# A mixture-of-experts encoder layer: experts with one block and with two taken in turn, in an order worked out on the chip

## The chip, the cores and the metric

The kernel runs on one core of one Trainium2 chip. The metric is the device time of one execution in microseconds (us). The engines are PE (TensorE: matrix products), DVE (VectorE), ACT (ScalarE), POOL (GpSimd) and SP (SyncE, which here only issues transfers); 16 DMA engines move data between HBM and the on-chip memories SBUF and PSUM.

## The reference

1024 tokens of width 1024 pass one layer: an RMSNorm, one projection `w_in`, two mixing branches (a spatial gating and a real 2-D Fourier transform), an output projection and the residual; then the experts, and a last RMSNorm. The part that matters here:

```
hn = rms_norm(h, norm2_g)
scores = sigmoid(hn @ w_router)                     # 64 experts
eidx, gates = top 8 of 64 per token, from the best 4 of 8 groups of experts
for every expert e: rows that chose it, padded to blocks of 128:
    out = (silu(xb @ w_gate[e]) * (xb @ w_up[e])) @ w_down[e] * gate
    y[tok] += out
h = h + y + shared expert(hn)
```

`w_gate[e]` and `w_up[e]` are 1024 x 256 and `w_down[e]` is 256 x 1024, all float32: 3 MB an expert, 192 MB for the 64. How many rows choose an expert depends on the input. With the inputs of the reference its routing gives every expert between 71 and 238 rows: 35 experts have up to 128 rows and so one block, 29 have more and so two, 93 blocks in all.

## The kernel before

**Three stages.** Up to about 345 us the dense part runs (projections, mixing, output projection, router scores). From there to about 457 us the tables of the experts are made, beside the shared expert. Then the expert stage takes the 93 blocks, here called items, one after the other, and after it the copies of the result are added and normalised.

**Tables (L1204 to L1282, L640 to L705).** DVE counts each expert's blocks (`nch`), PE adds them up over the experts with a triangular matrix (L688), and DVE derives for every item its expert and whether it is the first item of that expert. PE transposes these two columns (L692) and DVE writes them as rows 0 and 1 of `tab` (L1255, semaphore `s_tab`). Then for each of eight chunks of 128 tokens `slot_marks(c)` on DVE makes 8 `mark` and 8 `pick` tiles (L1263, L1265) in one of two buffers, and `table(c)` on PE multiplies them into the table of row numbers (L665); so `slot_marks(c)` waits for `table(c-2)`. Meanwhile PE does the shared expert: `s_gate_up(q, j)` (L648, eight pieces of 8 products) and `s_down(c)` (L658, eight pieces), with `shared_h(q)` on DVE between (L1137). `s_down(0)` waits for all four `shared_h` (semaphore `s_hm`). When the last `table` is through, DVE makes `idx_all` and `row_all` (L1280, L1282), which POOL's gathers wait for, and then takes the sums `y0(c)` (L1334); `s_down(c)` waits for `y0(c-2)`.

**Weights.** An expert's float32 weights are loaded by SP (L281, L282, L285) to `raw_gu` and `raw_dn`, each with two places. ACT makes a rounded copy (`split_gu`, L919, four parts; `split_dn`, L923, two parts), DVE the rest of it (`rest_gu`, L1144; `rest_dn`, L1151), into `w_gu` and `w_dn`, also with two places, taken in turn. Place 0 of `w_gu` lies where `xh` lies, from which `y0` is stored, so it is filled only after these stores. SP's order is fixed, whatever the blocks are: gate and up of expert e+1 (after expert e-1's are split), wait until expert e's have landed, down of expert e, wait for the landing of down of e-1, and on (L370 to L420). The loads of experts 0 and 1 are issued as soon as the output projection is done (L360), at about 347 us.

**One item i.** PE: transposes the gathered rows of i+1 (L464), `down(i-1)` (L735, 12 products), transposes h of i (L743), `gate_up(i+1)` (L721, 24 products). ACT and DVE do in item i: silu and gating, the two halves of the transposed rows (L934, L1297), and under `If`: the split of gate and up of the expert whose first item is i+2, and the split of down of the expert whose first item is i+1. So the weights are split at a fixed distance of items, and a place of `raw_gu` comes free two items before its expert is used. POOL gathers rows four items ahead (L1464), copies the gates (L1474) and adds the results to memory (L1492). Engines read `tab` into registers with `look` (L304), a `TENSOR_LOAD` and some register instructions.

Experts are taken by their number. With S for an expert of one item and D for one of two, this order is D S D D S S S D S D S D D S S D S S S S S D D D D D D D S S S S D S S D D D D S S S S S S S S D D D D S D S D S S D D D S S S S.

Of the kernel before, what the change touches and what calls it, by code (L numbers as in the profile page):

```python
# [31 lines left out]
NE = 64  # L32
# [5 lines left out]
KF = F // P  # L38
# [4 lines left out]
TAB = NITEM + 8  # L43
# [4 lines left out]
TURN = 3  # L48
GU_PARTS = 4
# [13 lines left out]
def build(nc, x, g1, w_in, ln_g, ln_b, wsT, bsT, ga, gb, w_out, g2, w_router, rbias, wg, wu, wd,  # L63
          sg, su, sd, dft_pos, dft_ch, gf, out, hn_d, y_d):
    ctx = ExitStack()
    with ctx:
        top = [nc.sbuf_base]

        def place(name, shape, dt, at=None):

            size = 2 if dt in (BF16, F16) else 4
            n = size
            for s in shape[1:]:
                n *= s
# [120 lines left out]
        tab = place("tab", [2, TAB], I32)  # L195
# [18 lines left out]
        def sem(name):  # L214
            return ctx.enter_context(nc.semaphore(name))
# [99 lines left out]
        def _(sp):  # L315
# [42 lines left out]
                sp.dma_start(hn_v[c, :, 0:D], rows[:, c % 2, :]).then_inc(s_hst[c % 2], 16)  # L358

            sp.wait_ge(s_wo, NC)  # L360
            for e in range(2):
                load_gu(sp, e, 1 - e)
                load_dn(sp, e, 1 - e)

            sp.wait_ge(s_gates, 1)
            sp.dma_start(gates_v[:, :, D:], rt_a[:, :, :]).then_inc(s_gst, 16)
            sp.wait_ge(s_gu_in[1], 32)
            sp.sem_inc(s_rg, 1)

            def load_next_gu(e, at):  # L370
                sp.wait_ge(s_hg, (e - 1) * GU_PARTS)
                sp.sem_inc(s_turn_sp, 1)
                sp.wait_ge(s_lg, (e - 1) * GU_PARTS)
                sp.sem_inc(s_turn_sp, 1)
                load_gu(sp, e, at)

            def load_next_dn(e, at):
                sp.wait_ge(s_hd, (e - 1) * KF)
                sp.sem_inc(s_turn_sp, 1)
                sp.wait_ge(s_ld, (e - 1) * KF)  # L380
                sp.sem_inc(s_turn_sp, 1)
                load_dn(sp, e, at)

            def gu_landed(at, fills):

# [74 lines left out]
        def _(pe):  # L460
# [223 lines left out]
            mm.then_inc(s_pm, 1)  # L684
            s_gate_up(0, 1)

            pe.wait_ge(s_chunks, 1)
            pe.matmul(ps[6][:, 0:NE], nchb[:, :], triI[:, :], start=True, stop=True).then_inc(s_pm, 1)  # L688
            s_gate_up(1, 0)

            pe.wait_ge(s_cols, 1)
            pe.matmul(ps[7][0:2, 0:P], cols[:, 0:2], ident[:, :], start=True, stop=True).then_inc(s_pm, 1)  # L692
            s_gate_up(1, 1)
            s_gate_up(2, 0)
            table(0)
            table(1)
            s_gate_up(2, 1)
            table(2)
            table(3)
            s_gate_up(3, 0)  # L700
            table(4)
            table(5)
            s_gate_up(3, 1)
            table(6)
            table(7)  # L705

            def turn_item(u, fills):

# [293 lines left out]
        def _(dv):  # L1002
# [218 lines left out]
            shared_h(0)

            dv.wait_ge(s_pm, 2)
            step(dv.tensor_copy(le[:, 2, :], ps[6][:, 0:NE]))
            step(dv.tensor_scalar(le[:, 0, :], le[:, 2, :], pidx[:, 0:1], None, ALU.is_le))
            step(dv.tensor_tensor(le[:, 1, :], le[:, 0, :], le[:, 2, :], ALU.mult))
            step(dv.tensor_reduce(cols[:, 2:3], le[:, 0, :], AX.X, ALU.add))
            step(dv.tensor_reduce(cols[:, 3:4], le[:, 1, :], AX.X, ALU.max))
            step(dv.tensor_scalar(cols[:, 0:1], cols[:, 2:3], float(NE - 1), None, ALU.min))
            step(dv.tensor_scalar(cols[:, 4:5], cols[:, 3:4], pidx[:, 0:1], None, ALU.is_equal))  # L1230
            step(dv.tensor_scalar(cols[:, 5:6], cols[:, 2:3], float(NE), None, ALU.is_lt))
# [4 lines left out]
            step(dv.tensor_scalar(ends[0:1, 0:1], ps[6][0:1, NE - 1:NE], 1.0, 1.0 / TURN, ALU.add, ALU.mult))  # L1236
# [4 lines left out]
            many((dv.memset(le[:, 3, 0:1], 0.0),  # L1241
                  dv.tensor_scalar(le[:, 3, 1:NE], le[:, 2, 0:NE - 1], float(P), None, ALU.mult)))
# [8 lines left out]
            many((dv.tensor_scalar(ends[:, 3:4], le[:, 2, NE - 1:NE], 1.0, 1.0 / TURN, ALU.add, ALU.mult),))  # L1251
            step(dv.tensor_copy(late[:, :], ends[:, 3:4]))
            step(dv.tensor_scalar(late[:, :], late[:, :], 1.0, float(TURN), ALU.subtract, ALU.mult))
            dv.wait_ge(s_pm, 3)
            dv.tensor_copy(tab[0:2, 0:P], ps[7][0:2, 0:P]).then_inc(s_tab, 1)  # L1255

            dv.wait_ge(s_info, 3)

            def slot_marks(c):

# [118 lines left out]
        def _(gp):  # L1379
# [205 lines left out]
```

## Time and profile before

| | us |
|---|---|
| three runs | 1404.11, 1408.82 (median), 1414.78 |
| the profiled execution, its own time | 1411.65 |
| its span, from the first to the last instruction | 1410.0 |
| busy in it: PE, DVE, ACT, POOL | 1309.5, 875.7, 738.1, 459.0 |

The span lies 1.65 us under the execution's own time. The profile's page lists busy times and the costliest groups of instructions; the chain of waits follows the work that ended last back from the end, in pieces; a piece such as "PE ps L721 x24" is a whole gate_up of one item. Stretches give busy times and DMA share between two times of the span.

### The profile page before, as it was taken

How to read it: one execution, taken by the hardware profiler on the slowest of the kernel's cores; microseconds unless marked ns; L12 is line 12 of the kernel's file. 1: busy time of each engine (PE TensorE's matmuls, PEld its weight loads, DVE VectorE, ACT ScalarE, POOL GpSimd, SP SyncE). 2: the span in 40 equal slices, each digit the busy share in tenths (PEclk: the TensorE clock that was granted, in tenths of full speed). 3: DMA queues.
4: the chain of work that ended last, by engine and by line, in shares of the span. 5: the costliest groups of instructions: out<-in, count | busy, mean ns of one | idle time of the engine just before them, and what ended most of it. 6: DMA issues, size and time to landing. Idle time of an engine off the chain costs nothing.

```text
span 1410.0 us, 25859 instructions
## 1 busy us (share of the span) xinstructions
PE 1309.5 (93%) x5960; PEld 1024.4 (73%) x5962; DVE 875.7 (62%) x1318; ACT 738.1 (52%) x1044; POOL 459.0 (33%) x608
## 2 busy tenths in 40 slices
PE   6899988999999999999989999999999999999960
PEld 5785466888444887888878888788877788888850
DVE  4430444345665676767866567776687666775846
ACT  4421244211011676767865657766677666775822
POOL 1431201000001344434443344334343434443435
PEclk9999999999999999999999999999999999999985
DMA  9464032002306799999999889999899989999987
GB/s 336 150 180 160 0 119 90 40 36 80 152 5 241 248 302 340 327 305 326 339 365 280 259 250 318 363 344 282 253 366 376 325 249 306 325 339 278 295 257 279
DMA packets 99535, 348.47 MB, mean 247 GB/s; under 512 B 13104, under 2 KB 33584, under 8 KB 82736
## 3 DMA queue, kind: packets, MB, share of 16 engines
q1 hardware_dynamic: 72144, 263.64, 48.7%
q0 software_dynamic: 27360, 84.44, 26.4%
q8 instruction: 16, 0.26, 0.1%
q14 instruction: 15, 0.12, 0.0%
HBM read 294.85 MB, written 71.57 MB: 260 GB/s over the span
## 4 chain that ended last, share of the span: by engine, by line
PE 71%; DMA 14%; ACT 3%; issue 3%; DVE 2%; POOL 1%; DVEq 1%; ACTq 1%; SPq 0%; POOLq 0%
PE ps L721 26%; PE ps_out L735 13%; DMA raw_gu<-in_w_up 8%; PE ps L613 6%; PE ps L481 5%; PE ps L464 5%; DMA raw_dn<-in_w_down 5%; PE ps L648 4%; PE ps L515 4%; PE ps L564 2%; ACT w_gu L919 1%; DMA y_rows_dram<-ob,idxs 1%; PE ps_out L630 1%; PE ps L743 1%; PE ps L658 1%
## 5 line engine op out<-in xcount | busy, mean ns | idle before, releaser
L721 PE MATMUL ps<-w_gu,xTh 128*128 x1504 | 477.9, 399 | 13.2 <-DVE xTl L1297 11.1
L1144 DVE TENSOR_TENSOR w_gu<-raw_gu,w_gu (+1 forms) x256 | 302.6, 1223 | 63.8 <-ACT w_gu L919 62.9
L721 PEld LDWEIGHTS ps<-w_gu,xTh 128*128 128x128 f32 x1504 | 279.0, 190 | 73.5 <-issue 19.3
L721 PE MATMUL ps<-w_gu,xTl 128*128 x752 | 296.6, 394 | 0.0
L919 ACT ACTIVATE w_gu<-raw_gu (+1 forms) x256 | 256.8, 1060 | 23.7 <-SPq L387 23.7
L735 PE MATMUL ps_out<-w_dn,hTh 128*128 x744 | 242.1, 407 | 0.0
L1492 POOL DMA_INDIRECT y_rows_dram<-ob,idxs x93 | 151.7, 1632 | 194.8 <-ACT ob L940 175.9
L1151 DVE TENSOR_TENSOR w_dn<-raw_dn,w_dn (+1 forms) x128 | 150.9, 1221 | 84.0 <-ACT w_dn L923 83.6
L721 PEld LDWEIGHTS ps<-w_gu,xTl 128*128 128x128 f32 x752 | 142.6, 190 | 30.0
L735 PEld LDWEIGHTS ps_out<-w_dn,hTh 128*128 128x128 f32 x744 | 133.1, 189 | 25.1
L735 PE MATMUL ps_out<-w_dn,hTl 128*128 x372 | 145.9, 392 | 0.0
L923 ACT ACTIVATE w_dn<-raw_dn (+1 forms) x128 | 128.4, 1057 | 31.8 <-SPq L391 31.6
L1297 DVE TENSOR_TENSOR xTl<-ps,xTh 128x512 fp32r<-128x512 f32 x188 | 120.9, 685 | 26.0 <-ACT xTh L934 26.0
L1464 POOL DMA_INDIRECT Xg<-hn_rows_dram,idxg x97 | 105.7, 1089 | 79.0 <-POOL idxg L1461 76.9
L1474 POOL COPY gate<-Xg 128x1 f32 x94 | 37.4, 398 | 287.6 <-PE ps L464 166.0
L934 ACT ACTIVATE xTh<-ps 128x512 fp32r<-128x512 f32 x188 | 102.3, 597 | 51.5 <-PE ps L464 51.5
L929 ACT ACTIVATE hs<-ps 128x256 f32<-128x256 f32 x93 | 35.7, 384 | 151.4 <-PE ps L721 151.0
L464 PEld LDWEIGHTS ps<-ident,Xg 128*128 128x128 f32 x752 | 98.0, 190 | 8.1 <-issue 0.5
L1412 POOL TENSOR_SCALAR rs<-ms 128x1 f32<-128x1 f32 x40 | 25.8, 645 | 239.9 <-ACT junk L789 238.3
L940 ACT ACTIVATE ob<-ps_out 128x1024 f32<-128x1024 f32 x93 | 95.1, 1022 | 7.0 <-PE ps_out L735 7.0
L464 PE MATMUL ps<-ident,Xg 128*128 128x128 f32 x752 | 98.3, 274 | 0.0
L1290 DVE SCALAR_TENSOR_TENSOR hh<-hs,gate,ps 128x256 f32<-128x256 f32 x93 | 44.6, 479 | 63.3 <-ACT hs L929 44.0
(206 smaller groups left out, 1554.8 us busy)
## 6 DMA issues: line engine op xcount, KB each, us to landing
raw_gu<-in_w_gate SPq DMA_DIRECT2D x64, 1024.0 KB, 7.5
raw_gu<-in_w_up SPq DMA_DIRECT2D x64, 1024.0 KB, 10.8
raw_dn<-in_w_down SPq DMA_DIRECT2D x64, 1024.0 KB, 14.8
y_rows_dram<-zero SPq DMA_DIRECT2D x1, 9216.0 KB, 37.6
x_ring<-in_x SPq DMA_DIRECT2D x8, 512.0 KB, 5.0
w_in_sb<-in_w_in SPq DMA_DIRECT2D x8, 512.0 KB, 9.7
xh<-in_x SPq DMA_DIRECT2D x8, 512.0 KB, 8.2
w_out_sb<-in_w_out SPq DMA_DIRECT2D x1, 4096.0 KB, 12.9
```

Source lines behind the costliest of these rows:

```text
L464: last = pe.transpose(ps[banks[k // 4]][:, (k % 4) * P:(k % 4 + 1) * P], src[:, k:D:KD], ident[:, :])
L721: mm = pe.matmul(ps[3][:, :], x_[:, k, :], w_gu[:, bass.ds(at, 1), part, :, k, :], start=(k == 0 and part == 0 and x_ is xTh), stop=(k == ...
L735: mm = pe.matmul(ps[6 + half][:, :], h_[:, k, :], w_dn[:, bass.ds(at, 1), part, k, half * 512:(half + 1) * 512], start=(k == 0 and part == ...
L919: act.activation(gu_part(w_gu[:, :, 0, :, :, :], at, m), gu_part(raw_gu, at, m), ACT.Copy).then_inc(s_hg, 1)
L923: act.activation(w_dn[:, bass.ds(at, 1), 0, k, :], raw_dn[:, bass.ds(at, 1), k, :], ACT.Copy).then_inc(s_hd, 1)
L934: act.activation(xTh[:, half * 4:half * 4 + 4, :], ps[1 + half][:, :].rearrange("p (k t) -> p k t", k=4), ACT.Copy).then_inc(s_xa, 1)
L940: act.activation(ob[:, u, :], ps_out[:, :], ACT.Copy).then_inc(s_oa, 1)
L1144: dv.tensor_tensor(gu_part(w_gu[:, :, 1, :, :, :], at, m), gu_part(raw_gu, at, m), gu_part(w_gu[:, :, 0, :, :, :], at, m).bitcast(F32), AL ...
L1151: dv.tensor_tensor(w_dn[:, bass.ds(at, 1), 1, k, :], raw_dn[:, bass.ds(at, 1), k, :], w_dn[:, bass.ds(at, 1), 0, k, :].bitcast(F32), ALU.s ...
L1297: dv.tensor_tensor(xTl[:, part, :], ps[1 + half][:, :].rearrange("p (k t) -> p k t", k=4), xTh[:, part, :].bitcast(F32), ALU.subtract).the ...
L1464: gp.indirect_dma_start(out=Xg[:, u, :], out_offset=None, in_=hn_d[:, :], in_offset=bass.IndirectOffsetOnAxis(ap=idxg[:, u:u + 1], axis=0) ...
L1492: gp.indirect_dma_start(out=y_d[:, :], out_offset=bass.IndirectOffsetOnAxis(ap=idxs[:, u:u + 1], axis=0), in_=ob[:, u, :], in_offset=None, ...
```

## The change

The order of the experts is worked out on the chip. DVE marks which experts have more than one block (`multi`), PE sums these marks, and DVE makes a key per expert that spreads both kinds evenly (`key_t`, `kinds`), and from the keys a matrix `upto` of who comes before whom, which takes the place of the triangular one. `tab` gets a third row, the number of the expert in place j. SP looks there before each load, and POOL looks there for the column of the gate, behind its look at row 0. All else goes by place j instead of expert e. For the inputs of the reference the order becomes

S D S D S D S D S D S S D S D S D S D S D S S D S D S D S D S S D S D S D S D S D S S D S D S D S D S D S S D S D S D S D S D S

with five places where two S stand together, and no two D together. Since the loads need row 2 of `tab`, those of the first two experts now wait for `s_tab`. PE's small products of the tables and the pieces of the shared expert stand in another order, and `shared_h(3)` on DVE stands ahead of the wait for the last table.

```
--- before.py
+++ after.py
             sp.wait_ge(s_wo, NC)
-            for e in range(2):
-                load_gu(sp, e, 1 - e)
-                load_dn(sp, e, 1 - e)
-
             sp.wait_ge(s_gates, 1)
             sp.dma_start(gates_v[:, :, D:], rt_a[:, :, :]).then_inc(s_gst, 16)
+            sp.wait_ge(s_tab, 1)
+            for j in range(2):
+                e = look(sp, 2, j, NE - 1)
+                load_gu(sp, e, 1 - j)
+                load_dn(sp, e, 1 - j)
...
-                load_gu(sp, e, at)
+                load_gu(sp, look(sp, 2, j, NE - 1), at)
...
-                load_dn(sp, e, at)
+                load_dn(sp, look(sp, 2, j, NE - 1), at)
...
+            pe.wait_ge(s_kinds, 1)
+            pe.matmul(ps[6][:, 0:NE], multi[:, :], tri[0:NE, 0:NE], start=True, stop=True)
+            pe.matmul(ps[6][:, NE:2 * NE], multi[:, :], identb[:, :], start=True, stop=True)
+            pe.matmul(ps[6][:, 2 * NE:2 * NE + 1], multi[:, :], ones[0:NE, 0:1], start=True, stop=True).then_inc(s_pm, 1)
+            s_gate_up(1, 0)
+
             pe.wait_ge(s_chunks, 1)
-            pe.matmul(ps[6][:, 0:NE], nchb[:, :], triI[:, :], start=True, stop=True).then_inc(s_pm, 1)
-            s_gate_up(1, 0)
+            pe.matmul(ps[7][:, 0:NE], nchb[:, :], upto[:, :], start=True, stop=True)
+            pe.matmul(ps[7][:, NE:2 * NE], nchb[:, :], identb[:, :], start=True, stop=True)
+            pe.matmul(ps[7][:, 2 * NE:3 * NE], ones[0:NE, :], upto[:, :], start=True, stop=True)
+            pe.matmul(ps[7][:, 3 * NE:3 * NE + 1], nchb[:, :], ones[0:NE, 0:1], start=True, stop=True).then_inc(s_pm, 1)
+            s_gate_up(1, 1)
...
-            for c in range(4):
+            s_down(0)
+            s_down(1)
+            table(6)
+            table(7)
+            for c in range(2, 6):
                 s_down(c)
             turn_item(0, 1)
-            for c in range(4, NC):
+            for c in range(6, NC):
                 s_down(c)
...
+            step(dv.tensor_tensor(identb[:, :], triI[:, :], tri[0:NE, 0:NE], ALU.subtract))
+            step(dv.tensor_scalar(pidx1[:, :], pidx[:, :], 1.0, None, ALU.add))
             dv.wait_ge(s_pm, 1)
+            step(dv.tensor_scalar(multi[:, :], ps[5][0:NE, 0:1].to_broadcast([NE, P]), float(P), None, ALU.is_gt))
+            dv.sem_inc(s_kinds, 1)
...
+            dv.wait_ge(s_pm, 2)
+            before, is_multi = ps[6][0:NE, 0:NE], ps[6][0:NE, NE:2 * NE]
+            n_multi, n_single = kinds[:, 0:1], kinds[:, 1:2]
...
+            many((dv.tensor_scalar(key_t[:, 0, :], key_t[:, 0, :], 0.5, n_multi, ALU.add, ALU.mult),
+                  dv.tensor_scalar(key_t[:, 1, :], before, 0.5, n_single, ALU.add, ALU.mult)))
...
+            step(dv.tensor_scalar(upto[:, :], key_t[:, 0, :], kinds[:, 3:4], None, ALU.is_ge))
+            dv.sem_inc(s_chunks, 1)
             shared_h(0)
...
+            shared_h(3)
             dv.wait_ge(s_table, NC)
...
             dv.tensor_tensor(row_all[:, :], idx_all[:, :], copy_row[:, :], ALU.add).then_inc(s_idx, 1)
-            shared_h(3)
...
-                e = look(gp, 0, i, NE - 1)
+                e = look(gp, 2, look(gp, 0, i, NE - 1), NE - 1)
```

PE, from the last small product of the tables to the first pieces of `s_down`, before (L648 is `s_gate_up`, L665 `table`, L658 `s_down`; a row of L665 x16 is two tables):

```order
L692 MATMUL ps_out<-ident,cols 2x128
L648 MATMUL ps<-T,sgu_w 128x512 x16
L665 MATMUL ps<-mark,pick 128x136 x16
L648 MATMUL ps<-T,sgu_w 128x512 x8
L665 MATMUL ps<-mark,pick 128x136 x16
L648 MATMUL ps<-T,sgu_w 128x512 x8
L665 MATMUL ps<-mark,pick 128x136 x16
L648 MATMUL ps<-T,sgu_w 128x512 x8
L665 MATMUL ps<-mark,pick 128x136 x16
L658 MATMUL ps<-sd_w,hsT 128x512 x4
L658 MATMUL ps_out<-sd_w,hsT 128x512 x4
```

The same place on PE after the change (L656, L673 and L666 are the same three functions):

```order
L709 MATMUL ps_out<-ident,cols 3x128
L656 MATMUL ps<-T,sgu_w 128x512 x16
L673 MATMUL ps<-mark,pick 128x136 x16
L656 MATMUL ps<-T,sgu_w 128x512 x8
L673 MATMUL ps<-mark,pick 128x136 x16
L656 MATMUL ps<-T,sgu_w 128x512 x8
L673 MATMUL ps<-mark,pick 128x136 x16
L666 MATMUL ps<-sd_w,hsT 128x512 x4
L666 MATMUL ps_out<-sd_w,hsT 128x512 x4
L673 MATMUL ps<-mark,pick 128x136 x16
L666 MATMUL ps<-sd_w,hsT 128x512 x4
L666 MATMUL ps_out<-sd_w,hsT 128x512 x4
```

The first pair of tables stands behind six of the eight pieces of `s_gate_up` instead of five; the last pair, which stood ahead of `s_down(0)`, stands behind `s_down(1)`, and no `s_gate_up` is left beside the last two `slot_marks`.

DVE, from the third `shared_h` (L1137) to the first `y0` (L1334), before:

```order
L1137 TENSOR_TENSOR hsT<-s_tmp,ps 128x512
L1263 TENSOR_SCALAR mark<-count_row,item_110,token 128x136 x8
L1265 TENSOR_SCALAR pick<-count_row,place_111 128x128 x8
L1263 TENSOR_SCALAR mark<-count_row,item_110,token 128x136 x8
L1265 TENSOR_SCALAR pick<-count_row,place_111 128x128 x8
L1277 TENSOR_SCALAR late_row<-count_row,late 128x136
L1278 TENSOR_TENSOR copy_row<-copy_row,late_row 128x136
L1280 TENSOR_SCALAR idx_all<-ps,dump 128x136
L1282 TENSOR_TENSOR row_all<-idx_all,copy_row 128x136
L1137 TENSOR_TENSOR hsT<-s_tmp,ps 128x512
L305 TENSOR_LOAD tab
L305 ISA x2
```

And after (L1155 is `shared_h`):

```order
L1155 TENSOR_TENSOR hsT<-s_tmp,ps 128x512
L1304 TENSOR_SCALAR mark<-count_row,item_110,token 128x136 x8
L1306 TENSOR_SCALAR pick<-count_row,place_111 128x128 x8
L1304 TENSOR_SCALAR mark<-count_row,item_110,token 128x136 x8
L1306 TENSOR_SCALAR pick<-count_row,place_111 128x128 x8
L1318 TENSOR_SCALAR late_row<-count_row,late 128x136
L1319 TENSOR_TENSOR copy_row<-copy_row,late_row 128x136
L1155 TENSOR_TENSOR hsT<-s_tmp,ps 128x512
L1322 TENSOR_SCALAR idx_all<-ps,dump 128x136
L1324 TENSOR_TENSOR row_all<-idx_all,copy_row 128x136
L312 TENSOR_LOAD tab
L312 ISA x2
```

The last `shared_h` moved ahead of `idx_all`, and still stands behind `slot_marks(6)` and `slot_marks(7)`.

## Rows read from the trace of the kernel before

**Rows 1.** The page: busy us of each engine, and one group of instructions (mean ns).

```profile
PE 1309.5 (93%) x5960; PEld 1024.4 (73%) x5962; DVE 875.7 (62%) x1318; ACT 738.1 (52%) x1044; POOL 459.0 (33%) x608
...
L1144 DVE TENSOR_TENSOR w_gu<-raw_gu,w_gu (+1 forms) x256 | 302.6, 1223 | 63.8 <-ACT w_gu L919 62.9
```

**Rows 2.** The chain of waits, expert stage: start us, us, what.

```profile
457.69 7.12 PE ps L721 x24
...
751.26 5.48 PE ps L721 x24
...
863.76 5.48 PE ps L721 x24
...
1010.76 5.46 PE ps L721 x24
...
1048.19 14.98 DMA raw_gu<-in_w_up
...
1117.00 5.74 PE ps L721 x24
...
1345.08 5.71 PE ps L721 x24
```

**Rows 3.** The chain of waits, where one and two items alternate.

```profile
565.76 5.50 PE ps L721 x24
...
575.17 5.73 PE ps L721 x24
...
594.19 5.46 PE ps L721 x24
...
613.24 5.46 PE ps L721 x24
...
1239.71 5.48 PE ps L721 x24
...
1259.10 5.48 PE ps L721 x24
```

**Rows 4.** Stretches: start:end length, busy of PE PEld DVE ACT POOL, PEclk, DMA share, GB/s.

```profile
565.00:622.00 57.00, 56.95 (x279) 47.15 (x278) 40.52 (x48) 38.47 (x53) 23.99 (x31) 1.00 0.97 311
751.00:864.00 113.00, 113.00 (x557) 94.36 (x556) 68.94 (x85) 69.45 (x99) 44.88 (x61) 1.00 0.89 262
1027.00:1113.00 86.00, 79.30 (x367) 64.29 (x366) 65.32 (x76) 62.34 (x83) 32.46 (x40) 0.96 1.03 370
```

**Rows 5.** Timeline, making the tables, PE, DVE: start us, us, engine, line.

```profile
393.05 1.11 PE L665 MATMUL ps<-mark,pick 128*128 128x136 f16 x16
393.73 1.89 DVE L1263 TENSOR_SCALAR mark<-count_row,item,token 128x136 f16<-128x136 f16 x8 [5.76 <-PE ps L665]
...
397.08 1.89 DVE L1263 TENSOR_SCALAR mark<-count_row,item,token 128x136 f16<-128x136 f16 x8 [0.16 <-DVE pick L1265]
...
418.27 0.30 DVE L1282 TENSOR_TENSOR row_all<-idx_all,copy_row 128x136 int32<-128x136 int32 x1
418.48 0.68 DVE L1137 TENSOR_TENSOR hsT<-s_tmp,ps 128x512 f32<-128x512 f32 x1
...
419.31 1.10 PE L658 MATMUL ps<-sd_w,hsT 128*128 128x512 f32 x2 [1.56 <-DVE hsT L1137]
```

**Rows 6.** The chain of waits from the last y0 to the first hh.

```profile
447.94 1.30 DVE xh L1334 x2
...
449.26 4.68 DMA y_rows_dram<-xh
...
454.99 0.31 DVEq L305
...
455.34 0.18 DVEq L305
```

**Rows 7.** Timeline of ACT and of DVE, a D behind an S.

```profile
606.51 2.01 ACT L923 ACTIVATE w_dn<-raw_dn  x2 [1.62 <-SPq L391]
...
610.89 0.69 DVE L1297 TENSOR_TENSOR xTl<-ps,xTh 128x512 fp32r<-128x512 f32 x1 [0.20 <-ACT xTh L934]
```

More of the change, by code:

```diff
@@ L168, in build @@
         gidx = place("gidx", [P, NC, 8], U32, M_AT + 3 * KB + 256)
+        key_t = place("key_t", [NE, 4, NE], F32, M_AT)
+        multi = place("multi", [NE, P], BF16, M_AT + 3 * KB + 768)
         late_row = place("late_row", [P, TAB], F32, M_AT + 3 * KB)
@@ L194, in build @@
         cols = place("cols", [P, 12], F32)
-        tab = place("tab", [2, TAB], I32)
+        tab = place("tab", [3, TAB], I32)
+        identb = place("identb", [NE, NE], BF16)
+        upto = place("upto", [NE, NE], BF16)
+        kinds = place("kinds", [NE, 4], F32)
+        pidx1 = place("pidx1", [P, 1], F32)
         ends = place("ends", [P, 8], I32)
@@ L246, in build @@
         s_mask, s_chunks, s_cols = sem("mask_ready"), sem("chunks_ready"), sem("item_cols_ready")
+        s_kinds = sem("kinds_ready")
         s_rv, s_pm, s_tab = sem("routing_step"), sem("routing_matmul"), sem("tables_ready")
@@ L685, in _ @@
             s_gate_up(0, 1)
-            pe.wait_ge(s_chunks, 1)
-            pe.matmul(ps[6][:, 0:NE], nchb[:, :], triI[:, :], start=True, stop=True).then_inc(s_pm, 1)
-            s_gate_up(1, 0)
+            pe.wait_ge(s_kinds, 1)
[3 more added lines that the diff above has]
+            s_gate_up(1, 0)
+            pe.wait_ge(s_chunks, 1)
+            pe.matmul(ps[7][:, 0:NE], nchb[:, :], upto[:, :], start=True, stop=True)
[3 more added lines that the diff above has]
+            s_gate_up(1, 1)
             pe.wait_ge(s_cols, 1)
-            pe.matmul(ps[7][0:2, 0:P], cols[:, 0:2], ident[:, :], start=True, stop=True).then_inc(s_pm, 1)
-            s_gate_up(1, 1)
+            pe.matmul(ps[6][0:3, 0:P], cols[:, 0:3], ident[:, :], start=True, stop=True).then_inc(s_pm, 1)
             s_gate_up(2, 0)
+            s_gate_up(2, 1)
             table(0)
             table(1)
-            s_gate_up(2, 1)
+            s_gate_up(3, 0)
             table(2)
             table(3)
-            s_gate_up(3, 0)
+            s_gate_up(3, 1)
             table(4)
             table(5)
-            s_gate_up(3, 1)
-            table(6)
-            table(7)
             def turn_item(u, fills):
@@ L1220, in _ @@
             dv.wait_ge(s_t3, NC)
+            dv.wait_ge(s_info, 3)
+            dv.wait_ge(s_pm, 2)
+            before, is_multi = ps[6][0:NE, 0:NE], ps[6][0:NE, NE:2 * NE]
+            n_multi, n_single = kinds[:, 0:1], kinds[:, 1:2]
+            many((dv.tensor_scalar(n_multi, ps[6][0:NE, 2 * NE:2 * NE + 1], 1.0, None, ALU.max),
+                  dv.tensor_scalar(kinds[:, 2:3], ps[6][0:NE, 2 * NE:2 * NE + 1], -1.0, float(NE), ALU.mult, ALU.add),
+                  dv.tensor_tensor(key_t[:, 0, :], count_row[0:NE, 0:NE], before, ALU.subtract)))
@@ new lines, in _ @@
+            step(dv.tensor_scalar(n_single, kinds[:, 2:3], 1.0, None, ALU.max))
+            many((dv.tensor_scalar(key_t[:, 0, :], key_t[:, 0, :], 0.5, n_multi, ALU.add, ALU.mult),
+                  dv.tensor_scalar(key_t[:, 1, :], before, 0.5, n_single, ALU.add, ALU.mult)))
+            step(dv.scalar_tensor_tensor(out=key_t[:, 1, :], in0=key_t[:, 1, :], scalar=0.25, in1=key_t[:, 0, :],
+                                         op0=ALU.add, op1=ALU.subtract))
+            step(dv.tensor_tensor(key_t[:, 1, :], key_t[:, 1, :], is_multi, ALU.mult))
@@ L1221, in _ @@
+            step(dv.tensor_tensor(key_t[:, 0, :], key_t[:, 0, :], key_t[:, 1, :], ALU.add))
+            step(dv.tensor_tensor(key_t[:, 2, :], key_t[:, 0, :], ident[0:NE, 0:NE], ALU.mult))
+            step(dv.tensor_reduce(kinds[:, 3:4], key_t[:, 2, :], AX.X, ALU.add))
+            step(dv.tensor_scalar(upto[:, :], key_t[:, 0, :], kinds[:, 3:4], None, ALU.is_ge))
+            dv.sem_inc(s_chunks, 1)
             shared_h(0)
-            dv.wait_ge(s_pm, 2)
-            step(dv.tensor_copy(le[:, 2, :], ps[6][:, 0:NE]))
+            dv.wait_ge(s_pm, 3)
@@ L1225, in _ @@
+            step(dv.tensor_copy(le[:, 2, :], ps[7][:, 0:NE]))
             step(dv.tensor_scalar(le[:, 0, :], le[:, 2, :], pidx[:, 0:1], None, ALU.is_le))
             step(dv.tensor_tensor(le[:, 1, :], le[:, 0, :], le[:, 2, :], ALU.mult))
+            step(dv.tensor_reduce(cols[:, 8:9], le[:, 0, :], AX.X, ALU.add))
+            step(dv.scalar_tensor_tensor(out=le[:, 0, :], in0=ps[7][:, 2 * NE:3 * NE], scalar=pidx1[:, 0:1],
+                                         in1=count_row[:, 0:NE], op0=ALU.is_equal, op1=ALU.mult))
@@ L1227, in _ @@
             step(dv.tensor_reduce(cols[:, 2:3], le[:, 0, :], AX.X, ALU.add))
             step(dv.tensor_reduce(cols[:, 3:4], le[:, 1, :], AX.X, ALU.max))
-            step(dv.tensor_scalar(cols[:, 0:1], cols[:, 2:3], float(NE - 1), None, ALU.min))
+            step(dv.tensor_scalar(cols[:, 0:1], cols[:, 8:9], float(NE - 1), None, ALU.min))
             step(dv.tensor_scalar(cols[:, 4:5], cols[:, 3:4], pidx[:, 0:1], None, ALU.is_equal))
-            step(dv.tensor_scalar(cols[:, 5:6], cols[:, 2:3], float(NE), None, ALU.is_lt))
+            step(dv.tensor_scalar(cols[:, 5:6], cols[:, 8:9], float(NE), None, ALU.is_lt))
@@ L1235, in _ @@
             dv.sem_inc(s_cols, 1)
-            step(dv.tensor_scalar(ends[0:1, 0:1], ps[6][0:1, NE - 1:NE], 1.0, 1.0 / TURN, ALU.add, ALU.mult))
+            step(dv.tensor_scalar(ends[0:1, 0:1], ps[7][0:1, 3 * NE:3 * NE + 1], 1.0, 1.0 / TURN, ALU.add, ALU.mult))
             many((dv.tensor_scalar(ends[0:1, 1:2], ends[0:1, 0:1], 1.0, None, ALU.subtract),
@@ L1239, in _ @@
                   dv.tensor_scalar(ends[0:1, 4:5], ends[0:1, 0:1], 2.0, None, ALU.subtract)))
-            many((dv.memset(le[:, 3, 0:1], 0.0),
-                  dv.tensor_scalar(le[:, 3, 1:NE], le[:, 2, 0:NE - 1], float(P), None, ALU.mult)))
+            step(dv.tensor_tensor(le[:, 3, :], le[:, 2, :], ps[7][:, NE:2 * NE], ALU.subtract))
+            step(dv.tensor_scalar(le[:, 3, :], le[:, 3, :], float(P), None, ALU.mult))
             step(dv.scalar_tensor_tensor(out=rt_b[:, :, :], in0=ps[4][:, :].rearrange("p (c e) -> p c e", c=NC),
@@ L1250, in _ @@
                                          op0=ALU.mult, op1=ALU.add))
-            many((dv.tensor_scalar(ends[:, 3:4], le[:, 2, NE - 1:NE], 1.0, 1.0 / TURN, ALU.add, ALU.mult),))
+            many((dv.tensor_scalar(ends[:, 3:4], ps[7][:, 3 * NE:3 * NE + 1], 1.0, 1.0 / TURN, ALU.add, ALU.mult),))
             step(dv.tensor_copy(late[:, :], ends[:, 3:4]))
             step(dv.tensor_scalar(late[:, :], late[:, :], 1.0, float(TURN), ALU.subtract, ALU.mult))
-            dv.wait_ge(s_pm, 3)
-            dv.tensor_copy(tab[0:2, 0:P], ps[7][0:2, 0:P]).then_inc(s_tab, 1)
-            dv.wait_ge(s_info, 3)
+            dv.wait_ge(s_pm, 4)
+            dv.tensor_copy(tab[0:3, 0:P], ps[6][0:3, 0:P]).then_inc(s_tab, 1)
             def slot_marks(c):
```

13 lines of the change are left out of this document (6 added, 7 removed).

## The prediction

> **What bounds the kernel now.** I read the page first: PE is busy for 1309.5 us of 1410.0, DVE for 875.7 [rows 1]. So a gain must come from PE's waits, and next I looked for them in the chain of waits, whose pieces "PE ps L721 x24" are one gate_up per item. The expert stage runs from the gate_up of item 1 at 457.69 to that of item 92 at 1345.08: 887.39 us for 91 items [rows 2]. In the run of seven D, 12 items take 863.76 - 751.26 = 112.50 us, 9.375 each: this is PE's own pace, with matmuls and nothing else in the chain. 91 items at that pace are 853.1 us, so 34.3 us of the stage are waits. The reader is to see where: from 1010.76 to 1117.00, the end of a D and the eight S behind it, ten items take 106.24 us instead of 93.75, 12.5 too many, and there a DMA of 14.98 us on raw_gu stands in the chain [rows 2]. An S asks for 3.15 MB of weights in 9.4 us, a D in 18.8.
>
> The stretches say the same of the DMA engines [rows 4]: 370 GB/s at a share of 1.03 in the run of S, 262 at 0.89 in the run of D, 311 at 0.97 where they alternate. From the run of D, 262 GB/s x 18.75 us = 4.91 MB a D, of which 1.77 belong to the rows of two items, 0.885 each. A pair S D then moves 6.29 + 3 x 0.885 = 8.95 MB; at the 370 GB/s of the run of S that is 24.2 us, while PE needs 28.1 for its three items. So an alternating order should be bound by PE. Where before it does alternate, the trace agrees: an S and the D behind it take 594.19 - 565.76 = 28.43 us, 0.30 over three paces, the gate_up at 575.17 lasting 5.73 instead of 5.46 [rows 3].
>
> **The expert stage after.** There are 29 D; the first holds items 1 and 2, and 28 follow an S behind item 2. Terms:
> - 91 items at 9.375: 853.1 us.
> - The gate_up at 457.69 takes 7.12 us instead of 5.5 [rows 2]; PE had waited before it. It stays: 1.6.
> - The 0.30 us of a D behind an S. I put it on DVE: where both split jobs fall in one item there are six parts of 1.22 us [rows 1], two xTl of 0.69 [rows 7], and hh and hTl of some 0.45, together 9.6 us against a pace of 9.375. The change keeps it: 28 x 0.30 = 8.4.
> - Two S together, five places. The one at 1239.71 has the same neighbours (S D S S D); its two items take 19.39 us to 1259.10 [rows 3], 0.64 over two paces, so 0.34 more than the usual 0.30: 5 x 0.34 = 1.7.
> - SP's new looks. One costs 0.31 + 0.18 us with its gaps, 0.53, on DVE [rows 6]; SP's is not shown. The loads that have slack hide it. The tight one is the down of a D behind an S, for which ACT waits: at 606.51 it is released by SP's landing [rows 7]. SP issues this down just after the next gate and up, so it queues behind 2 MB in the same queue, and I count one look, not two. There the second xTl ends near 612.2 and PE wants it at 613.24 [rows 3, 7], so here 0.53 us would be hidden. Bounds per D: 0, and 1.06 if both looks reach PE; nearest to the row is 0, but landings vary, so I take 0.15: 4.2.
> Sum 869.0 us, against 887.4: 18.4 us saved. POOL's second look costs nothing here: it falls where POOL waits for PE's transposes. ACT, PE and DVE look at rows 0 and 1 as before.
>
> By the Trainium skill, "DMA: Bandwidth & Descriptors", section "Latency and other measured facts", loading registers has a floor near 600 ns. The look of 0.53 us on DVE lies a little under it; at 0.6 the 4.2 us of the looks would become at most some 2 us more.
>
> **The start of it.** Here the change costs time, on PE's path.
> - Small products: seven and one more stop for three and a wait. They delay the last s_gate_up by about 1.3 us (bounds 0.5 and 3), and the next term starts from that one's end, so they count in full.
> - s_down(0) waits for the last shared_h, which DVE does behind slot_marks(6) and (7). Before, these two ran beside the last s_gate_up, since the tables stood one piece of it earlier. Now slot_marks(6) starts only behind table(4), itself behind the last s_gate_up. A table pair to its mark is 393.73 - 393.05 = 0.7 us, a slot_marks is 397.08 - 393.73 = 3.35 [rows 5]. So from the start of the last pair before s_down: 0.7 + 2 x 3.35 + 0.65 (late_row, copy_row) + 0.85 (shared_h and its semaphore, 418.48 to 419.31) = 8.9 us. Before, the last pair ended one idx_all (0.36) ahead of row_all at 418.27, so it began near 416.7, and s_down(0) came at 419.31 [rows 5], 2.7 later. With the 1.3: PE starts s_down(0) 7.5 us later.
> - Between s_down(1) and s_down(2) PE now has tables 6 and 7 (1.1) and waits for y0(0), which stands behind idx_all, row_all (0.4 + 0.3), a look (0.5) and is itself 1.3 long [rows 5, 6], with semaphores 2.7: 1.1 + 2.7 = 3.8 us.
> - PE's wait of some 7 us lowers its clock, as before the gate_up at 457.69: 1.6 us, bounds 0 and 3.
> - Item 1 is now an expert's first. Behind the stores of y0 (4.68 us [rows 6], as before) DVE has four rest_gu of 1.22 to do before hh of item 0: 4.8 us.
> Sum 7.5 + 3.8 + 1.6 + 4.8 = 17.7 us; from 13 (the clock does not fall, half of the four parts hidden) to 22. The loads of the first two experts, some 41 us later than before (behind s_tab, at about 388 instead of 347), land by some 410 and are split from about 418: hidden. DVE's steps for the key, some 3 us, lie beside an s_gate_up of 7: hidden.
>
> **Sum.** 17.7 - 18.4 = -0.7. Against the profiled execution's own 1411.65 that gives 1410.9; the median of the runs is 2.8 under it, so 1408 us. The gain in the expert stage is paid back in the 60 us ahead of it.
>
> **Rivals.**
> 1. The queue cannot hold the alternation, slower. The place is the down of every D behind an S. For it: share 0.97 at only 311 GB/s [rows 4]; if the engines are full at that rate with this mix, a pair's 8.95 MB take 28.8 us, already over the 28.43 of PE. Against it: 370 in the run of S. It decides from the point where a landing is later than DVE's margin of about 1 us; then each D pays both looks, 28 x 1.06 = 29.7 in place of 4.2, and the stage gains nothing: 1408 + 25 = 1433 us.
>  The skill's page on DMA, section "Where 436 GB/s comes from", puts a core's HBM limit near 358 GB/s. The run of S shows 370, and by either the pair would fit.
> 2. The start is mostly hidden and the 0.30 us go, faster. For it: in the run of D nothing is paid, and it could have been the gate copy, not DVE's work, that cost 0.30. Then the stage is 18.4 + 8.4 + 4.2 = 31 us shorter, and the start costs 13: 1411.65 - 2.8 - 18 = 1391 us. Against it: PE's order shows the wait plainly.
> 3. It does not do what it says: the waits of the stage stay, because what ends them is latency (issue to landing) rather than bytes. Only the start's 17.7 is left: 1409 + 18 = 1427 us. Against it: the alternating rows 3 already run at PE's pace.
>
> **How the numbers follow.** Forecast 0.70, rival 1 0.13, rival 2 0.10, rival 3 0.07. A measurement of this kernel tells about 1% (14 us) from no change. The forecast's own range is 1399 to 1420 (start 13 to 22, looks 0 to 15). Faster by over 1%: rival 2 and a little, 0.11. Slower by over 1%: rivals 1 and 3, 0.19. Within 1%: 0.70. The range that is to hold 8 in 10 reaches 1397 to 1427.
>
> **What would show it.** Right: PE starts s_down near 427 behind a wait of about 8 us for hsT; the gate_up of item 1 starts near 475; from there to item 92's it is 865 to 873 us; no DMA on raw_gu in the chain in the stage. Wrong: gate_ups of D's second items with waits of 0.5 to 1 us each on xTl (rival 1); s_down before 422 (rival 2); stretches of 11 to 12 us an item (rival 3).

## The result and the profile after

| | before | after |
|---|---|---|
| median of the runs, us | 1410.87 (1404.11 to 1415.56, 18 runs) | 1414.71 (1410.65 to 1416.68, 18 runs) |
| ratio, 95% interval | | 1.0027 (1.0017 to 1.0037) |
| span of the profiled execution, us | 1410.0 | 1414.9 |
| gate_up of item 1 starts | 457.69 | 474.70 |
| from there to gate_up of item 92 | 887.4 | 875.4 |

The change makes the kernel 3.8 us slower, a small loss with an interval clear of no change; I had forecast a gain of 0.7. The time lies within the forecast's 1399 to 1420; the direction is wrong. S and D are experts of one and of two items, as in the prediction. Of an item's steps, hs and xTh are ACT's (silu, and its half of the transposed rows), hh and xTl are DVE's (the gating, and its half). The page answers to [rows 1]:

```profile
PE 1309.4 (93%) x5966; PEld 1024.2 (72%) x5968; DVE 880.5 (62%) x1335; ACT 739.5 (52%) x1044; POOL 450.4 (32%) x608
...
L735 PE MATMUL ps<-w_gu,xTh 128*128 x1504 | 474.5, 397 | 12.3 <-DVE xTl L1338 10.1
...
L937 ACT ACTIVATE w_gu<-raw_gu (+1 forms) x256 | 256.6, 1057 | 23.9 <-SPq L395 17.7
```

The last two rows are new reading. PE waits 10.1 us in all for xTl ahead of its gate_ups, and ACT waits 17.7 us for SP at L395, the wait in gu_landed: SP's flag that an expert's gate and up weights have landed.

The chain of waits at the start, with what answers to [rows 5, 6]:

```profile
425.83 6.26 PE ps L666 x8
432.09 3.43 PE ps_out L666 x8
435.52 0.96 PE ps L673 x16
436.51 0.37 DVE idx_all L1322
...
437.84 1.30 DVE xh L1375 x2
439.19 3.70 PE ps L666 x8
...
462.29 5.10 DMA y_rows_dram<-xh
...
472.81 0.39 DVE hh L1331
473.20 1.21 DVE xTl L1338 x2
...
474.70 7.67 PE ps L735 x24
```

s_down(0) starts at 425.83 behind 7.75 us of waiting. Its eight products take 6.26 us, in the stretches (columns as in [rows 4]) at a granted clock of 0.58, between the two levels and near the lower, against 3.70 at 1.00 for the eight of s_down(2):

```profile
425.83:432.09 6.26, 6.26 (x9) 2.69 (x10) 0.00 (x0) 0.00 (x0) 0.00 (x0) 0.58 0.01 3
439.19:442.89 3.70, 3.70 (x9) 1.79 (x10) 3.41 (x4) 0.00 (x0) 2.60 (x4) 1.00 0.72 215
```

Between s_down(1) and (2) lie tables 6 and 7, idx_all and y0(0), 435.52 to 439.19.

In the stage the chain has no DMA on raw_gu any more; in the whole chain DMA holds 2%. The stretch of the alternation answers to [rows 4]:

```profile
565.00:622.00 57.00, 55.84 (x274) 46.24 (x272) 40.65 (x48) 40.09 (x55) 22.85 (x29) 1.00 0.97 313
```

PE idles 1.16 us of these 57, where before it idled 0.05 in the same stretch at nearly the same GB/s. The two stretches do not hold the same items, but what PE waits for here is no transfer, as the chain shows. It is shown at one S and the D behind it:

```profile
640.97 5.46 PE ps L735 x24
...
650.33 5.48 PE ps L735 x24
...
658.28 0.47 DVE hh L1331
658.75 1.21 DVE xTl L1338 x2
```

and the timeline one item earlier, where the D's gate and up are split:

```profile
646.47 0.39 ACT L947 ACTIVATE hs<-ps 128x256 f32<-128x256 f32 x1 [2.27 <-PE ps L735]
...
647.35 1.09 ACT L952 ACTIVATE xTh<-ps 128x512 fp32r<-128x512 f32 x2 [0.50 <-PE ps L472]
...
647.80 0.34 SPq L288 DMA_DIRECT2D raw_gu<-in_w_gate  x1
...
648.24 0.51 SPq L289 DMA_DIRECT2D raw_gu<-in_w_up  x1
...
649.15 2.01 ACT L937 ACTIVATE w_gu<-raw_gu  x2 [0.71 <-SPq L395]
```

ACT is done with xTh at 648.44 and waits 0.71 us for SP's flag. SP raises it only after it has issued the next expert's load, and that issue comes behind the wait for the previous split and the new look: in the trace SP's wait for the split ends at 646.08, its register load lasts from 646.24 to 647.34, 1.10 us, and the flag is raised at 648.88. So ACT's split starts 2.68 us behind hs; it starts 1.86 behind hs where it does not wait. DVE's six parts follow ACT's, so they end later, hh and xTl of the next item too, and PE pays. Over the stage, from hs of item 1 to hs of item 92 (this measure serves below; before 886.0 us, after 873.2), the interval in which DVE finishes a D's parts and which ends in hs of the D's first item takes 9.86 us on the mean, not the forecast's 9.375 + 0.30 = 9.67.

### The profile page after: what moved, and what is told of

It is laid out like the page before. It is cut to its first block, busy times and chain, and to the rows that moved or that the text cites. A ratio compares the mean times of both kernels' runs of the same rounds, so it can differ in the third digit from the quotient of the medians.

```text
span 1414.9 us, 26783 instructions
## 1 busy us (share of the span) xinstructions
PE 1309.4 (93%) x5966; PEld 1024.2 (72%) x5968; DVE 880.5 (62%) x1335; ACT 739.5 (52%) x1044; POOL 450.4 (32%) x608
## 4 chain that ended last, share of the span: by engine, by line
PE 72%; issue 7%; DVE 5%; ACT 3%; DVEq 2%; DMA 2%; POOL 2%; SPq 2%; ACTq 2%; POOLq 0%
PE ps L735 28%; PE ps_out L749 12%; PE ps L621 6%; PE ps L472 5%; PE ps L489 5%; PE ps L656 4%; PE ps L523 4%; ACT w_gu L937 2%; PE ps L572 2%; DVE xTl L1338 2%; DVE w_gu L1162 1%; DMA y_rows_dram<-ob,idxs 1%; PE ps L666 1%; PE ps_out L638 1%; SPq L312 1%
## 5 line engine op out<-in xcount | busy, mean ns | idle before, releaser
L735 PE MATMUL ps<-w_gu,xTh 128*128 x1504 | 474.5, 397 | 12.3 <-DVE xTl L1338 10.1
L937 ACT ACTIVATE w_gu<-raw_gu (+1 forms) x256 | 256.6, 1057 | 23.9 <-SPq L395 17.7
L1515 POOL COPY gate<-Xg 128x1 f32 x94 | 33.5, 356 | 289.1 <-PE ps L472 152.5
```

Of the source, the lines that this page charges most:

```text
L735: mm = pe.matmul(ps[3][:, :], x_[:, k, :], w_gu[:, bass.ds(at, 1), part, :, k, :], start=(k == 0 and part == 0 and x_ is xTh), stop=(k == ...
L937: act.activation(gu_part(w_gu[:, :, 0, :, :, :], at, m), gu_part(raw_gu, at, m), ACT.Copy).then_inc(s_hg, 1)
```

## The experiments

Stage means hs of item 1 to hs of item 92 in the profiled execution; each is one execution, and the same kernel's may differ by 2 us and more. Times are medians of 4 to 12 runs (18 for before and after), ratios are to runs of before made beside them.

| kernel | stage | hs of item 1 | median | ratio, 95% |
|---|---|---|---|---|
| before | 886.0 | 464.9 | 1410.9 | 1 |
| after | 873.2 | 482.4 | 1414.7 | 1.0027 (1.0017 to 1.0037) |
| e1 flags first | 863.7 | 481.8 | 1404.9 | 0.9964 (0.9951 to 0.9977) |
| e2 look early | 863.6 | 480.6 | 1405.7 | 0.9976 (0.9955 to 0.9997) |
| e3 by number | 887.3 | 479.0 | 1426.2 | 1.0106 (1.0078 to 1.0134) |
| e4 shared_h early | 875.1 | 473.8 | 1405.5 | 0.9963 (0.9947 to 0.9979) |
| e5 by number, flags first | 891.4 | 476.4 | 1429.4 | 1.0119 (1.0100 to 1.0138) |
| e6 = e1 + e2 + e4 | 863.5 | 473.5 | 1397.8 | 0.9898 (0.9882 to 0.9914) |
| e7 = e6, DVE's looks late | 861.5 | 472.6 | 1393.5 | 0.9872 (0.9848 to 0.9896) |
| e8 two looks | 892.0 | 481.4 | 1434.6 | 1.0156 (1.0136 to 1.0176) |
| e9 = e7, surplus S last | 861.4 | 471.6 | 1393.3 | 0.9871 (0.9852 to 0.9889) |
| e10 = e7, y0(0) first | 869.3 | 471.0 | 1392.2 | 0.9869 (0.9846 to 0.9893) |
| e11 gate/up flag only | 864.0 | 481.3 | 1406.2 | 0.9969 (0.9952 to 0.9987) |
| e12 down flag only | 875.1 | 481.2 | 1415.4 | 1.0034 (1.0020 to 1.0047) |

**e1: SP's flags ahead of the next load.**

```diff
-                load_next_gu(t * 2 + 1, 0)
                 gu_landed(1, t + 1)
-                load_next_dn(t * 2, 1)
+                load_next_gu(t * 2 + 1, 0)
                 dn_landed(0, t)
+                load_next_dn(t * 2, 1)
```

(and so in the loop's other half and behind it)

> After, with SP raising the flag of a landed expert (gate/up, and down) ahead of the wait, look and issue of the next load instead of behind them. Expert stage of after (hs of item 1 to hs of item 92) 873.2 us; the item in which two-block experts are split takes 9.86 on the mean. Theory F (the flag, late by SP's look behind the split's end, holds ACT's and DVE's splits): ACT no longer waits for the flag, that item falls to 9.7 or less, stage to 862-869, kernel 4 to 10 us below after. Rival Q (the weights themselves land too late in an alternation): the flag waits for the landing, stage stays within 2 us of 873. Rival V (VectorE's own six parts and its own look hold the item): stage stays within 2 us too, but ACT's waits for SP vanish.

Measured: stage 9.5 us shorter, the item 9.66 on the mean. ACT's idle time ahead of the split of gate and up, and PE's ahead of the gate_up:

```profile
L735 PE MATMUL ps<-w_gu,xTh 128*128 x1504 | 474.9, 397 | 4.1 <-DVE xTl L1338 3.8
...
L937 ACT ACTIVATE w_gu<-raw_gu (+1 forms) x256 | 256.7, 1060 | 6.2 <-DMA y_rows_dram<-xh 6.2
```

The 17.7 us on SP are gone and PE waits 3.8 us for xTl instead of 10.1. Theory F holds. Q falls, since the flag could be raised at once, and V falls, since the stage got shorter with ACT's waits.

**e2: the look ahead of the waits.**

```diff
             def load_next_gu(j, at):
+                e = look(sp, 2, j, NE - 1)
                 sp.wait_ge(s_hg, (j - 1) * GU_PARTS)
...
-                load_gu(sp, look(sp, 2, j, NE - 1), at)
+                load_gu(sp, e, at)
```

(load_next_dn likewise)

> After, with SP reading the expert's number ahead of the two waits for the splits instead of behind them; flag still behind the issue of the load. Theory F with the look as the price: the flag comes earlier by the look (1.1 us where it is long), stage 863-870, nearly all of what e1 gives. If it is the order of flag and load and not the look: a third of e1's gain or less. Rival Q: nothing (within 2 us of 873). A gain here and none in e1 would say that the loads were issued late, not the flag.

Measured: the same 9.6 us. So it is the look on the flag's path that costs. Before had the same order of load and flag and no look, and its two issues alone fit ahead of ACT, as at this place of its own alternation, the same kind of item as the one shown of after:

```profile
590.14 0.34 SPq L281 DMA_DIRECT2D raw_gu<-in_w_gate  x1
590.32 0.39 ACT L929 ACTIVATE hs<-ps 128x256 f32<-128x256 f32 x1 [2.29 <-PE ps L721]
590.58 0.42 SPq L282 DMA_DIRECT2D raw_gu<-in_w_up  x1
...
592.18 2.00 ACT L919 ACTIVATE w_gu<-raw_gu  x2
```

There the flag is raised at 591.05, 1.14 us behind the end of the wait at 589.91, and the split starts 1.86 us behind hs without waiting. At the place shown of after it is 2.80 us (646.08 to 648.88).

**e11 and e12: which flag.** Each makes half of e1's edit, e11 that of gu_landed, e12 that of dn_landed. The prediction had put the price on down.

> e1's edit for the gate/up flag alone; the flag of down stays behind the issue of the next down. The prediction priced SP's looks on the path of down; theory F puts them on the flag of gate and up. Theory F: this half gives nearly all of e1's 9.5 us: stage 862-866, ACT's 17.7 us of waits for the gate/up flag gone. Rival D (the prediction's path, down): stage 870-873.

> e1's edit for the flag of down alone; the flag of gate and up stays behind the look and the issue of the next gate/up. Theory F: stage within 2 us of 873, ACT's waits for the gate/up flag stay at 15-20 us. Rival D (the prediction's path, down): stage 862-866.

Measured: 864.0 and 875.1. The flag of gate and up gives all of it, that of down nothing. ACT's rows of e12, where the wait stays:

```profile
L937 ACT ACTIVATE w_gu<-raw_gu (+1 forms) x256 | 256.6, 1057 | 23.8 <-SPq L395 17.8 <-DMA y_rows_dram<-xh 6.0
```

and the timeline of e11 at the place shown of after:

```profile
642.78 0.39 ACT L947 ACTIVATE hs<-ps 128x256 f32<-128x256 f32 x1 [2.57 <-PE ps L735]
...
644.64 2.01 ACT L937 ACTIVATE w_gu<-raw_gu  x2
```

The split starts 1.86 us behind hs, with no idle time ahead of it.

**e8: the dose doubled.**

```diff
+                look(sp, 0, j, NE - 1)
                 load_gu(sp, look(sp, 2, j, NE - 1), at)
```

(and so ahead of the look for down)

> After with a second look (row 0 of the table, unused) ahead of the one in each of SP's later loads, all else as after. Theory F (a look on the way to the flag delays it by its own length, and the landing has nothing to do with it): the flag of a two-block expert 0.3 later where the first look took the long part, up to 0.7; the item in which it is split 10.1-10.4 instead of 9.86; stage 881-888, kernel 8 to 15 above after. Rival (the look's price was only its long form, 1.1 us, which ends when the transposes end, whatever stands ahead of it): the short second look fits in, stage 873-877.

Measured: 892.0, 18.8 us more than after, and the median 19.8 more: above my range. PE's waits for xTl grow from 10.1 to 25.5 us, and ACT is idle for 41 us ahead of the splits of gate and up, apart from the stores of y0, where it was 17.7 in after:

```profile
L737 PE MATMUL ps<-w_gu,xTh 128*128 x1504 | 474.7, 397 | 26.6 <-DVE xTl L1340 25.5 <-ACT w_gu L939 0.9 <-issue 0.2
...
L939 ACT ACTIVATE w_gu<-raw_gu (+1 forms) x256 | 256.6, 1056 | 47.8 <-issue 21.5 <-SPq L397 19.3 <-DMA y_rows_dram<-xh 7.0
```

By hs the price seems to fall elsewhere than expected: the D's item takes 9.98 instead of 10.1 to 10.4, and an S behind a D 10.0 instead of 9.4. But hs of that S is itself late here, since ACT is still splitting: it starts 0.82 us behind PE's transposes instead of 0.26. Counted on PE, from the start of one item's transposes to the next (90 intervals), nearly all of it is paid at one kind of place, the 28 intervals in which PE comes to the expert behind the first S after a D (23 times a D, 5 times a second S). They exceed 9.375 us each by 3.9 us in all in e1, by 18.5 in after and by 35.4 in e8: 0.52 a place for the first look and 0.60 for the second. The split of gate and up, 1.85 us behind hs in e1, starts 2.56 behind it in after and 3.13 in e8 (medians at these items), so of the first look's delay about 0.2 us is absorbed and of the second's nothing. The stage shows less for the first, 9.5 us, because all other intervals together exceed the pace by 1.5 us in after and by 6.6 in e1, nearly all of it behind two S, where down weights land late.

**e3 and e5: the order alone.** The key becomes the expert's number, and everything else of after stays; e5 has e1's flags as well.

```diff
-            step(dv.tensor_tensor(key_t[:, 0, :], key_t[:, 0, :], key_t[:, 1, :], ALU.add))
+            step(dv.tensor_tensor(key_t[:, 0, :], count_row[0:NE, 0:NE], count_row[0:NE, 0:NE], ALU.max))
```

> After with the sort key replaced by the expert's number: the same table, looks, products and start, but experts in the order of before. Theory (the order saves, the machinery costs): start stays 17 us later than before, stage goes back from 873 to 886 plus what the looks of SP cost there (0 to 15 us): kernel 12 to 30 us slower than after, 1427 to 1445. Rival (the order saves nothing, and the stage of after is shorter for another reason): within 3 us of after.

> After with the key replaced by the expert's number (as e3) and the flags first (as e1). Measured so far: stage of before 886.0, after 873.2, e1 863.7, e3 887.3. Theory (the look's price falls where two-block experts stand behind others that leave slack; the order itself is worth over 20 us once SP is out of the way): stage 883-887, so the order is worth 20-23 with the flags first against 14 without; kernel 15 to 20 above before. Rival (flag first helps every order alike): stage 876-880, order worth 13-16, kernel 5 to 10 above before.

Measured: 887.3 and 891.4. The order is worth 14.1 us with the flags as in after and 27.7 with them first. Both expectations had the sign. e3 is 11.5 us slower than after, a little under the expected 12 to 30; e5's figure of 20 to 23 for the order was too small, its stage longer than the expected 883 to 887, and the flags, worth 9.5 in the alternation, are worth nothing by number (4.1 worse in one execution each, and 3.2 in the medians). An order by number is held more by transfers than the alternation. In the chain of e3 they hold 15%, 7.0% on raw_gu and 6.1% on raw_dn, against 2% in after; with the flags first it is 17% (e5) against 9% (e1). That in e5 the next load's issue waits for the landing of the one before, and that this costs the 4, was not tried by itself.

**e4: the last shared_h earlier.**

```diff
                 if c == 5:
                     shared_h(2)
+                    shared_h(3)
...
-            shared_h(3)
```

> After with VectorE's last part of the shared expert's hidden values, shared_h(3), right behind shared_h(2) and ahead of the marks of tables 6 and 7. Theory (those marks and late_row stand on the path of the first down product): s_down(0) starts at 418.5-419.5 instead of 425.8, its eight products take 3.6-4 instead of 6.3, and gate_up of item 1 starts 7 to 9 us earlier than 474.7; kernel 7 to 9 below after. Rival (the tables 6, 7 and the y0 evacuations then come last and eat it): 0 to 4 us.

Measured: gate_up of item 1 starts 8.9 us earlier, hs of item 1 8.6, the median falls by 9.3. Its chain:

```profile
417.47 3.67 PE ps L666 x8
421.14 3.43 PE ps_out L666 x8
424.57 0.96 PE ps L673 x16
425.63 0.37 DVE idx_all L1322
...
428.31 5.40 PE ps L666 x8
```

s_down(0) is 8.4 us earlier, more than expected, and takes 3.67 us. The clock falls one wait later now: behind 2.79 us of waiting the products at 428.31 take 5.40 at a granted 0.68, where after's s_down(2), behind 2.71 us of waiting, had 3.70 at 1.00. So part of the clock's price only moved along, and the length of the wait just ahead does not tell it alone.

**e6: the three together.**

> After with e1, e2 and e4 together: flags first, look ahead of the waits, shared_h(3) early. If the gains of e1 (stage 9.5) and e4 (start 8.6) add and e2 is the same gain as e1: stage 862-864, hs of item 1 at 472-474, kernel 1395 to 1398, ratio to before 0.989-0.991. Rival (what e1 and e2 give are two different gains): stage 854-857, kernel under 1391.

Measured: 863.5 and 473.5, median 1397.8: the gains of e1 and e4 add, e2's is the same as e1's.

**e7: DVE's own looks out of the way.**

```diff
-                ahead = expert(i + 2)
                 gated_h(i, u)
                 rest_xT(i + 1)
+                ahead = expert(i + 2)
...
+                if coming is None:
+                    coming = expert(i + 1)
                 with dv.If(coming[0] > 0):
```

(and the call at the turn's beginning goes)

> e6 with VectorE's own looks moved: the look for item i+2 behind the gate and the split of xT instead of ahead of them, and the second look of a turn's first item just before the down parts that need it. In e1, hh started at +1.76 after hs where one look stood ahead of it and the item took 9.40; it started at +1.99 to +2.08 at some 10 items that begin a turn (two looks ahead) and these took 9.64 to 9.73. Theory (those looks are the whole of it): these items fall to 9.4, stage 2 to 4 us below e6. Rival (VectorE is full over the two items, so moving changes nothing): within 1 us of e6.

Measured: stage 2.0 us shorter, at the low end. Nearly all of the turns' first items fell to 9.40 to 9.45, as expected (one stayed at 9.66), and hs of item 1 came 1.0 us earlier. The medians say 4.3 less, of intervals that overlap. What is left stands behind two S. In its chain, ahead of the first item of the D behind the fourth such pair (hs of item 61 to hs of item 62: 12.35 us):

```profile
1020.21 0.34 SPq L288
1020.64 0.89 SPq L289
...
1023.10 13.01 DMA raw_dn<-in_w_down
...
1037.32 12.03 DMA raw_dn<-in_w_down
```

and this stretch beside one of plain alternation, columns as in [rows 4]:

```profile
1024.00:1052.00 28.00, 28.00 (x139) 23.30 (x137) 19.02 (x22) 18.95 (x27) 11.96 (x15) 1.00 1.02 346
1080.00:1108.00 28.00, 28.00 (x139) 23.33 (x138) 19.74 (x24) 19.62 (x27) 12.18 (x15) 1.00 0.97 310
```

There three experts are loaded in 28 us, 346 GB/s at a full share, and the down weights land late.

**e9: no two S together but at the end.** In the key's scale the two ALU.max become ALU.min.

> e7 with the experts spread otherwise: strictly one of one block, one of two, and the surplus of one-block experts at the end (two max in the key's scale become min). In e7 the six items over 9.6 us in the stage (9.60, 10.65, 10.24, 12.35, 9.91 and an early one of 9.66) are first items of a two-block expert behind two one-block ones, and the down weights' DMA stands in the chain there. Theory L (three loads in 28 us: the third lands late at those places): they fall to 9.4 and the stage to 855-858 unless the six at the end pay; stage 855-860, kernel 1 to 6 below e7. Rival (six one-block experts in a row outrun the queue more than five places of two did): items at the end 9.8-10.5, stage 861-866.

Measured: 861.4, the rival. The five places are gone, but the last items between hs of items 75 and 92 now take 9.88, 12.17, 10.63, 10.75 and 9.93. The chain there is of transfers:

```profile
1282.35 12.13 DMA raw_gu<-in_w_up
...
1296.03 8.71 DMA raw_gu<-in_w_up
...
1306.13 9.74 DMA raw_gu<-in_w_up
```

In these two placements, by one profiled execution each, the surplus of S costs the same.

**e10: y0(0) ahead of the tables' end.** The four lines of idx_all and row_all move behind y0(0).

> e7 with VectorE's first evacuation of the shared expert, y0(0), ahead of the wait for the tables 6 and 7. In e4 and e6 the third down product waits from the tables' end (424.67+0.96) through idx_all, row_all, a look and y0(0) to 428.40. Theory: that wait goes, gate_up of item 1 starts 2.0 to 2.8 us earlier, kernel 2 to 3 below e7. Rival (the stores of y0, which hold VectorE at 453-458 there, or the gather of the first items takes it back): under 1 us.

Measured: hs of item 1 is 1.6 us earlier, short of the expected 2.0 to 2.8, and the median is 1.3 under e7's with intervals that overlap: not settled. Its profiled execution had a stage of 869.3, with 12.7, 12.4 and 12.3 us at items behind two S. Its time, 1401.15, is 9 over the median of its runs, and the chain has DMA on raw_dn at these places: the late landings vary from execution to execution.

## Why the prediction was wrong

- **The start.** Forecast 17.7 us later, measured 17.0. s_down(0): 7.5 against 6.5. The clock: 1.6 against 2.6. Tables and y0(0) between s_down(1) and (2): 3.8 against 3.7. Item 0's four rest_gu: 4.8 against about 4.2 left over; in e3, where item 1 is no expert's first, gate_up(1) starts 3.1 us earlier. The largest terms are what they were called, as e4 shows: with shared_h(3) moved, 8.9 of the 17.0 go. The sum is nearer than its terms, and that is luck: from the last pair of tables to s_down(0) it is 8.86 us, as forecast (8.9), but the pair starts only 0.3 us later than before (416.97 against 416.65) and not 1.3, and the clock's price is 1.0 too low.
- **The order.** The alternation is bound by PE and not by the queue, as rival 1 denied: no raw_gu in the chain, 313 GB/s, and the order alone is worth 27.7 us with the flags first (e1 against e5, one profiled execution each). The argument from 8.95 MB a pair held.
- **The step that failed: SP's looks, "I take 0.15: 4.2".** They cost 9.5 us of the stage (e1, e2), 0.34 per D, more than twice that; at the 28 places themselves it is 0.52 each, of which late landings elsewhere hide a part (e8). I followed one of the two things that SP's look delays. The prediction took the landing of down for the tight one and counted one look against a margin of about 1 us, and said that loads with slack hide the other. But SP does not only issue transfers, as was said at the start: it also passes on their landing as a flag. And gu_landed stands behind load_next_gu, so the look delays the flag of an expert whose weights are long there, and ACT and through it DVE wait for the flag, not for the load. e11 and e12 decide between the two: 9.2 us to the one, nothing to the other. Moreover the register load there mostly takes 1.1 us and not the 0.31 of DVE's row.
- **The sum.** Measured by gate_up, the stage was 6.4 us longer than forecast (875.4 against 869.0): 5.3 of it is the looks' excess, 0.6 the first gate_up at 7.67 instead of 7.12. The start came 0.7 better. Together these make 5.7 us, and the difference between -0.7 and the 4.9 us by which the spans differ is 5.6; hence slower and not a little faster. The bounds of the looks (0 to 29.7) held the truth; the value was chosen by a margin on the wrong path.
- **The two S together, 0.34 at five places.** Too low: in e7 the intervals that are left there, 9.60 to 12.35, exceed the pace by about 6 us. It was not what failed, since in after the other wait hides part of it.
- **The 0.30 of a D behind an S.** In e7 these items take 9.43 in the median, 9.65 in the mean with the late landings. Of the forecast 8.4 us no more than some 2 is DVE's fixed work; the rest is looks of DVE, ahead of hh at a turn's beginning, and landings. That this term and the last still add up is luck: forecast 8.4 + 1.7 = 10.1; on PE (as counted at e8) e1 shows 3.9 at the 28 places and 6.6 elsewhere, nearly all behind two S.
- The scenario of rival 2 (the start hidden) and of rival 3 (the stage does not move) did not come.

## What to carry to other kernels

When an instruction is added to a sequencer, list every signal that it raises behind that point and not only the transfer that it issues: a flag for work that was done long ago can be the one that pays. Raise such a flag ahead of the next wait, and read a table before a wait instead of behind it; each of the two gave 9.5 us here, and both together no more (e6). And follow the step that a reordering leaves last: a few moved lines (e1, e2 and e4 together, e6) turned 3.8 us slower into 13 us faster.

## What the runs showed of the hardware

A register load has two lengths. Of SP's 122 in the stage of after, 32 take over 0.6 us (median 1.10), the others about 0.28; DVE has 23 long of 122. PE has them too, 30 of 153. Of SP's 32 long ones 23 start 0.22 to 0.25 us ahead of an hs, as PE goes over to transposing the gathered rows, and end about when that does: one lasts from 646.24 to 647.34, the transposes beside it from 646.27 to 647.31. With the looks ahead of the waits (e2) SP has 5 long ones of 121; with DVE's behind hh and xTl DVE has 1 (e7) instead of 25 (e6). ACT and POOL have none. That moving a look out of this window shortens it is shown; what in the window holds it wasn't tried.

Before, the Trainium skill, "DMA: Bandwidth & Descriptors", section "Latency and other measured facts", was quoted for a floor near 600 ns for loading registers. By these rows most take 0.28 us, half of that, and a quarter of SP's nearly double; the measurement decides. The prediction set a whole look, 0.53 us, beside that figure; the register load in it is the 0.31 of [rows 6].
